# Norm and step sizes in one stage of a Trainium2 kernel, with three projection pieces moved into it from attention

## What is computed

```
h = rmsnorm(x);  P = h @ W_in                       # one projection, split into
q, k, v, z, xbc, dt_f, dt_b, gate_a, gate_s = split(P)
a = W_a( windowed GQA(q, k, v) with QK norm, rotary, a sink logit per head )
s = W_s( gated RMSNorm( bidirectional SSD scan of conv(xbc), step sizes softplus(dt + bias) ) )
x = x + W_o( sigmoid(gate_a) * a + sigmoid(gate_s) * s )
x = x + top-2-of-8 experts in the top-1-of-4 group ( rmsnorm(x) )
```

## Time and profile before

| | us |
|---|---|
| median of 3 runs | 2020.5 |
| lowest, highest | 2015.5, 2022.53 |
| the profiled execution, whole time | 2021.15 |
| its span in the trace | 2019.3 |
| TensorE busy in it | 1816.7 (90%) |
| mean granted TensorE clock | 0.947 of full |

### The profile page before, as it was taken

How to read it: one execution, slowest core, us unless ns; L and a number is a source line. 1 busy time by engine, 2 the same in 40 slices (tenths; PEclk the granted TensorE clock), 3 DMA queues, 4 the chain that set the end, 5 groups by cost and what they waited for, 6 DMA issues and landing times. The chain is left out here.

```text
span 2019.3 us, 26351 instructions
## 1 busy us (share of the span) xinstructions
PE 1816.7 (90%) x9522; PEld 1435.8 (71%) x9522; DVE 1305.0 (65%) x1359; ACT 1021.0 (51%) x1593; POOL 660.7 (33%) x374
## 2 busy tenths in 40 slices
PE   4888998999899989899999898985999999999992
PEld 3777887887778765577778787773677777777771
DVE  2686875884886671734344446315888888888884
ACT  4243533444354343166676422222677777777871
POOL 5147637555764871300034432311010011100100
PEclk7899999999999998899999999886999999999996
DMA  3242433435335343311156463334899999999995
GB/s 112 67 123 81 128 105 98 120 107 146 100 105 142 112 139 143 99 51 58 61 157 195 142 211 107 118 139 151 317 358 371 369 378 366 377 375 371 368 354 197
DMA packets 228111, 379.51 MB, mean 188 GB/s; under 512 B 14576, under 2 KB 176624, under 8 KB 203312
## 3 DMA queue, kind: packets, MB, share of 16 engines
q1 hardware_dynamic: 220272, 363.45, 52.5%
q0 software_dynamic: 7168, 12.60, 1.8%
q10 hardware_dynamic: 576, 2.18, 0.3%
HBM read 333.94 MB, written 55.25 MB: 193 GB/s over the span
## 5 line engine op out<-in xcount | busy, mean ns | idle before, releaser
L2064 DVE TENSOR_TENSOR e_w_low<-e_raw,e_w_high 128x2048 fp32r<-128x2048 f32 x190 | 426.5, 2285 | 62.1 <-ACT e_w_high L2060 62.1
L523 POOL TENSOR_TENSOR w_w_low<-w_raw,w_w_high 128x1024 fp32r<-128x1024 f32 x92 | 252.6, 2746 | 452.1 <-ACT w_w_high L518 452.1
L185 PE MATMUL bank<-h_high,w_w_high 128*128 128x256 f32 x960 | 338.0, 352 | 31.9 <-ACT ssd_conv_in L802 16.7
L2060 ACT ACTIVATE e_w_high<-e_raw 128x2048 fp32r<-128x2048 f32 x190 | 349.7, 1914 | 0.0
L185 PE MATMUL bank<-h_low,w_w_high 128*128 128x256 f32 x960 | 329.0, 343 | 0.0
L185 PE MATMUL bank<-h_high,w_w_low 128*128 128x256 f32 x960 | 328.3, 342 | 0.0
L185 PEld LDWEIGHTS bank<-h_high,w_w_high 128*128 128x128 f32 x960 | 188.1, 196 | 66.4 <-issue 30.7
L2076 PE MATMUL bank<-e_w_high,e_xT_high 128*96 128x512 f32 x512 | 206.6, 404 | 3.2 <-DVE e_xT_low L2157 1.6
L946 DVE SCALAR_TENSOR_TENSOR ssd_xc<-ssd_conv_in,ssd_conv_p,ssd_xc 128x774 f32<-128x774 f32 x144 | 196.3, 1364 | 10.8
L2076 PE MATMUL bank<-e_w_high,e_xT_low 128*96 128x512 f32 x512 | 203.3, 397 | 0.0
L2076 PE MATMUL bank<-e_w_low,e_xT_high 128*96 128x512 f32 x512 | 202.3, 395 | 0.0
(11 more groups left out here) (296 smaller groups left out, 3600.3 us busy)
## 6 DMA issues: line engine op xcount, KB each, us to landing
e_raw<-in_w_gate SPq DMA_DIRECT2D x64, 1024.0 KB, 7.4
e_raw<-in_w_up SPq DMA_DIRECT2D x64, 1024.0 KB, 7.6
e_raw<-in_w_down SPq DMA_DIRECT2D x64, 1024.0 KB, 6.8
w_raw<-in_w_in SPq DMA_DIRECT2D x68, 512.0 KB, 3.9
ssd_decays<-decay_sums SPq DMA_DIRECT2D x48, 512.0 KB, 6.2
projected<-ssd_side SPq DMA_DIRECT2D x36, 384.0 KB, 2.5
w_raw<-in_w_out_ssm SPq DMA_DIRECT2D x16, 512.0 KB, 4.1
y_ssd<-ssd_y SPq DMA_DIRECT2D x24, 256.0 KB, 2.4
```

The costliest lines, as they stand in the source:

```text
L185: last = pe.matmul(out, lhs[k][a], rhs[k][b], start=(k == 0 and m == 0), stop=(k == n - 1 and m == 2))
L523: pool.tensor_tensor(self.pair[u].low[:, :, :], self.raw[u][:, :, :], self.pair[u].high[:, :, :].bitcast(F32), ALU.subtract).then_inc(self ...
L2060: act.activation(pair[n].high[:, :], core.raw[c][:, :], ACT.Copy).then_inc(high_ok, 1)
L2064: dve.tensor_tensor(pair[n].low[:, :], core.raw[c][:, :], pair[n].high[:, :].bitcast(F32), ALU.subtract).then_inc(low_ok, 1)
```

## The change

`norm_and_transpose` and `step_sizes` become one stage, `front`. Three side pieces (`FRONT` = 3, the first three by number) are multiplied in it.

- The piece order begins with these three, then xbc of group 0, and goes on as before: the scan keeps 9 side pieces a group, each three numbers further on. `ATT_SIDES` falls from 8 to 5, so attention has 15 units: nine in the opening, six in the loop.
- SyncE issues six piece loads behind the loads of x and of the step sizes' weights.
- The norm loop: VectorE scales two tiles ahead, not one, and makes the low part of the second half of each tile; GpSimd makes the first half's. The transposes use four banks in turn, not eight. ScalarE rounds the step sizes' weights after tile 0 and one piece after each of tiles 1, 2 and 3. GpSimd makes six pieces' low parts after the loop.
- TensorE: all transposes, the two products of the step sizes (in one bank, the second waits for the copy of the first), the short half of piece 0, the six small transposes, the short halves of pieces 1 and 2, the chunk sums (they wait for the copies of all three short halves), the long half of piece 0, and, after the sums have left their banks, those of pieces 1 and 2.
- `a` is made ahead of the clipped `log_dt`.
- In attention the four stores of zeros go out together after the third side piece, not after the third to sixth.

The core of the diff (what only renumbers pieces in the scan, and the semaphores' names, is left out):

```
-SIDES, LAST_SIDES = 9, 9
-SSD_SIDES = (SG - 1) * SIDES + LAST_SIDES
+FRONT, SIDES, LAST_SIDES = 3, 9, 9
+SSD_SIDES = FRONT + (SG - 1) * SIDES + LAST_SIDES
...
             @block.sync
...
                 sp.dma_start(core.w_dt[:, :, :], core.w_in_cols(DT0, 2 * SH)).then_inc(core.w_dt_in, 16)
+                for n in range(2 * RING):
+                    load_piece(sp, core, n)
+                for n in range(FRONT):
+                    sp.wait_ge(first_left, n + 1)
+                    sp.wait_ge(second_left, n + 1)
+                    sp.dma_start(core.projected[n * P:(n + 1) * P, :], side[n][:, :]).then_inc(side_out, 16)
+                    if n == FRONT - 2:
+                        sp.wait_ge(sumT_ok, 2)
+                        for d in range(2):
+                            sp.dma_start(core.sums[d], sumT[:, d, :]).then_inc(sumT_out, 16)
...
+            @block.tensor
...
+                def steps(s):
+                    if s:
+                        pe.wait_ge(dtT_ok, s)
+                    pe.wait_ge(w_low_ok, 1)
+                    pe.wait_ge(first_low_ok, FIRST[s] + TILES[s])
+                    pe.wait_ge(second_low_ok, FIRST[s] + TILES[s])
+                    products(pe, core.bank[4][0:H2, 0:SEQS[s]], weights, h_parts(core, FIRST[s] * P, SEQS[s]))\
+                        .then_inc(dtT_mm, 1)
...
+                for t in range(NT):
+                    transposes(t)
+                for s in range(2):
+                    steps(s)
+                first(0)
+                for t in range(NT):
...
+                    last = pe.transpose(core.bank[0][:, t * H2:(t + 1) * H2], dtT[:, t * P:(t + 1) * P],
+                                        core.ident[0:H2, 0:H2])
+                last.then_inc(dt_mm, 1)
+                for n in range(1, FRONT):
+                    first(n)
+                pe.wait_ge(a_ok, 1)
+                pe.wait_ge(first_left, FRONT)
...
+                second(0)
+                pe.wait_ge(sumT_ok, 2)
+                for n in range(1, FRONT):
+                    second(n)
...
             @block.scalar
...
+                    if t == 0:
+                        act.wait_ge(core.w_dt_in, 16)
+                        act.activation(w_pair.high[:, :, :], core.w_dt[:, :, :], ACT.Copy).then_inc(w_high_ok, 1)
+                    if 0 < t <= FRONT:
+                        round_piece(act, core, t - 1)
...
             @block.gpsimd
...
-                    for j in range(2):
-                        pool.wait_ge(high_ok, 2 * t + j + 1)
-                        at = (slice(None), slice(4 * j, 4 * j + 4), slice(t * P, (t + 1) * P))
-                        pool.tensor_tensor(core.h.low[at], hT[j][:, :, :], core.h.high[at].bitcast(F32),
-                                           ALU.subtract).then_inc(low_ok, 1)
+                    pool.wait_ge(high_ok, 2 * t + 1)
+                    at = (slice(None), slice(0, 4), slice(t * P, (t + 1) * P))
+                    pool.tensor_tensor(core.h.low[at], hT[0][:, :, :], core.h.high[at].bitcast(F32),
+                                       ALU.subtract).then_inc(first_low_ok, 1)
+                for n in range(2 * FRONT):
+                    lower_piece(pool, core, n)
...
             @block.vector
...
-                scaled(0)
+                for t in range(2):
+                    scaled(t)
                 for t in range(NT):
-                    if t + 1 < NT:
-                        scaled(t + 1)
                     for j in range(2):
...
+                    if t + 2 < NT:
+                        scaled(t + 2)
+                    dve.wait_ge(high_ok, 2 * t + 2)
+                    at = (slice(None), slice(4, 8), slice(t * P, (t + 1) * P))
+                    dve.tensor_tensor(core.h.low[at], hT[1][:, :, :], core.h.high[at].bitcast(F32),
+                                      ALU.subtract).then_inc(second_low_ok, 1)
...
-                    if 2 <= i < 2 + D // ZW:
-                        zeros(i - 2)
+                    if i == 2:
+                        for c in range(D // ZW):
+                            zeros(c)
```

More of the change, by code:

```diff
@@ L222, in refined_root, with front @@
     return dve.tensor_tensor(out, out, part, ALU.mult)
-def norm_and_transpose(core):
+def front(core):
     nc = core.nc
@@ L274, in _ @@
                                        ACT.Copy).then_inc(high_ok, 1)
+                    if t == 0:
[3 more added lines that the diff above has]
+                        round_piece(act, core, t - 1)
+                act.activation(rate[:, :], core.row[:, R_ALOG:R_ALOG + H2], ACT.Exp).then_inc(rate_ok, 1)
+                for s in range(2):
+                    step_parts(s)
+                leave_first(0)
+                act.wait_ge(raw_ok, 1)
+                act.activation(low[:, :, :], low[:, :, :], ACT.Exp)
+                act.drain()
+                act.activation(low[:, :, :], low[:, :, :], ACT.Ln, bias=core.ones[:, 0:1]).then_inc(soft_ok, 1)
+                act.wait_ge(dt_ok, 1)
+                act.activation(tab["log_dt"], tab["log_dt"], ACT.Ln)
+                for n in range(1, FRONT):
+                    leave_first(n)
+                act.wait_ge(exp_in_ok, 1)
+                for name in ("reach", "to_end", "decay"):
+                    last = act.activation(tab[name], tab[name], ACT.Exp)
+                last.then_inc(exp_ok, 1)
+                for n in range(FRONT):
+                    leave_second(n)
             @block.gpsimd
@@ L703, in scan @@
                     store(g, NT - 1)
-                for n in range(RING, GC + 2 * RING):
+                for n in range(2 * RING, FRONT + GC + 2 * RING):
                     load_piece(sp, core, n)
@@ L789, in _ @@
                 pe.sem_inc(y_mm, NT)
-                for n in range(GC):
+                for n in range(FRONT, FRONT + GC):
                     project(n, n % RING)
@@ L850, in scan @@
                             leave_side(g, sides[n], n)
-                act.sem_inc(left, 2)
+                act.sem_inc(left, 2 + 2 * FRONT)
                 act.wait_ge(pads_ok, 1)
                 for ct in range(GC):
-                    leave(ct, ct, ct)
-                    round_piece(act, core, ct + RING)
+                    leave(FRONT + ct, ct, ct)
+                    round_piece(act, core, FRONT + ct + RING)
                     if 0 < ct < GC - 1:
```

238 lines of the change are left out of this document (105 added, 133 removed).

## The result

The changed kernel takes 2026.52 us (median of 20 runs, 2020.38 to 2031.16) against 2020.39 (20 runs) before; the ratio is 1.0021, interval 1.0012 to 1.0031: 4 us slower by 2 to 6. A second comparison, made beside the experiments, gave 1.0014 (0.9999 to 1.0029). The forecast was 2021 us in a range from 2011 to 2029, and no difference beyond 0.3%. The time lies in the range, 5.5 us above the forecast, and the difference is under 0.3%: 3 to 4 us, where the sum of the forecast had 0.3.

A forecast was written before the change was run, and what follows sets the result against it. TensorE, busy for 90% of the span, was taken as the bound, so a change pays where it idles. From 2021.15, +12.5 (front), -15.4 and +3.2 (attention) made 2021.5; forecast 2021 us, range 2011 to 2029.

The forecast's parts named there:

- The norm loop: Front: about 3.0 to 3.6 us a tile without contention; with 0.5 to 1.1 charged, last low part at 35.0.
- The collision: Norm loop: VectorE's and GpSimd's low parts of a tile contend for SBUF, charged 0.5 to 1.1 us a tile.
- the fourth rival: Front: pieces late, norm loop over 3.5 us a tile, short halves misfit; front +17 to +20, 2027 us; chance 0.12.
- The step sizes: Front: bias add at 44.4 us, sums start at 50.5 and take 4.4 at full clock, ending at 54.9.
- the tail: Front, after the last long half: copy, rounding, low part and border, 5.0 us, before the scan's first projection at 76.3.
- The clock fall between the two products: Front, step sizes: a bound, not expected; 2.7 us more if the clock falls there.
- The loop: Attention's loop of 24 groups, g0 to g23: gives back 12.2 us, from -15.4 and +3.2.
- The half-clock groups: Attention's g1 and g2, without a unit until g3: 7.5 us each at half clock; g1 to g3 +3.2 in all.
- The other groups: Attention groups losing a unit or a piece's end, apart from g1 to g3: give back 15.4 us.
- The clock did not come back by itself: Rival, attention: full clock returns in g1 or g2 without a unit, 5 to 8 us less, about 2013; chance 0.18.
- The slower rival: Attention: clock falls in stretches without units, 8 us for one (2029), 2045 and more if in all; chance 0.1.
- the forecast's +12.5 and -12.2: Scan's first projection 12.5 us later, at 76.3 instead of 63.77; attention gives back 12.2 us.

The follow-up runs named there:

- the first unit moved: Changed kernel with the attention loop's first unit in g1 instead of g3: ratio to the kernel before 0.9985, 2018.74 us.
- the low parts moved: Changed kernel with both low parts of a tile on GpSimd again: ratio to the kernel before 1.0009.
- the zeros spread: Changed kernel with the four stores of zeros one by one after attention's second to fifth side piece: ratio to the kernel before 1.0022.
- attention alone: Kernel before with only the change's attention, 5 side pieces and 15 units, three pieces not computed: ratio to the kernel before 0.9936.
- one edit away: Changed kernel with one of the loop's six units moved into the wait at the end of attention's opening: ratio to the kernel before 1.0072.
- the two runs of one side alone: Kernel before with only the change's attention, 0.9936; changed kernel with eight side pieces in attention again, 1.0059; both ratios to the kernel before.

## Why the prediction was right, and where it was off

**The norm loop.** I had the last low part at 35.0 and the second product at 35.1; it began at 34.26. The collision was there, at 1.66 us for VectorE's part against 0.69 with GpSimd idle, and in the shape forecast: GpSimd finishes and VectorE waits for it. The last tile shows it bare: GpSimd's part takes 1.27 us, as alone, and VectorE's, begun 0.55 later, ends 0.55 after it. GpSimd's 1.66 in the tiles before goes with something that I did not have: VectorE's scaling is running when GpSimd's part begins (21.78 to 22.52 against 22.00), and in the last two tiles, where no scaling is left, it takes 1.30 and 1.27. The Trainium skill's sentence on the shared SBUF interfaces (GPSIMD Engine Reference, "Key points") agrees with the rows of the two subtractions. The period was 3.55 us for the tiles with a scaling and 3.19 for the last two; so the first condition of the fourth rival (over 3.5) was met, and its price was not. As a reason against the edit it was sound: the split gained 0.5 to 0.8 us in the traces and nothing that shows in the timed runs.

**The step sizes.** Bias add 44.4 forecast, 43.41 measured; sums at 50.5, 49.88; 4.4 us at full clock, 4.2. (I had read half of the old 6.6 us as at half clock; their mean clock was 0.63, so about 4.9 us were, which makes 4.2.) The long halves took 16.6 us where I had 16.4, and the tail 4.64 where I had 5.0 with the last copy's lag. All terms but the first were within 0.4; the front as a whole was 0.9 too long. The clock fall between the two products, kept as a bound of 2.7 us, happened in two of the other traces (bias add at 45.2 and 45.4), and cost 1.8 to 2.

**The loop.** -12.0 measured, -12.2 forecast, from two errors that cancel. The half-clock groups were priced too low: 7.5 each forecast, 8.59 and 8.24 measured, near the upper bound of 8.6 that I had from twice the work. That it came near the bound is chance: the work did not double. TensorE was busy for 7.59 us of g1 and waited 1.00 for VectorE's maximum. My 7.5 took g0, added 1.5 for what it lacked, and left out the waits: g0 was busy for 5.46, so it lacked 2.1, and waited for 0.23. g3 was 8.91, not 9.73. So the three groups cost +4.2 and not +3.2. The other groups then gave back 16.2 and not 15.4; g6 and g22, priced at 6.0, came at 5.80, and g12 at 6.38 gave back 1.64 as priced.

**The rivals.** The clock did not come back by itself: 30.7 us at half clock in the changed kernel's loop and the scores ahead of it, from 858 to 888.7, of which TensorE was busy for 28.2. The Trainium skill's picture of activity that releases the clock (TensorE: Matmul & The Clock Gate, "What's actually happening") has to be read with this beside it: the clock rose in the unit of g3, and not before. The slower rival, a fall of the clock in the stretches without units, did not show in any trace with the changed kernel's places of the units: its two, and those with the first unit moved, the low parts moved, the zeros spread, and attention alone. It came one edit away, and not by the length of the stretch, which I had named: beside a group in which TensorE waited twice (in two traces, and not in six others with the same waits). The length then set what it cost. The pieces came in time, as the hole of 0.56 us shows.

**The difference that is left.** By the first pair of traces front and loop make -0.4 us. That pair flatters the change: it sets one of the slower traces of the kernel before beside the fastest front of the changed one. Over all traces the scan's first projection is at 63.1 us with the old front (62.1 to 63.9, four traces) and at 76.1 with the new one and its pieces (75.4 to 77.3, six), and the loop takes 164.1 with the old attention (five) and 152.8 with the new (five): +13.0 and -11.3, together +1.7. So the forecast's +12.5 and -12.2 are each within 1 us here too. By the two runs of one side alone 0.9936 x 1.0059 = 0.9995 (from their ends, 0.9957 x 1.0076 and 0.9915 x 1.0042, between 0.9957 and 1.0033), and the change measured 1.0021 and 1.0014. These agree within their intervals, and the middle of them is 1 to 3 us above the +1.7 of the traces. The places where the first pair of traces had it, opening and output stage, do not hold it in the repeated traces, where the opening of the changed kernel is the shorter one (88.0 against 92.2). A fall of the clock in the loop in some executions would be such a cost, but no trace of the changed kernel has one, nor has its loop the meeting of a piece's end and an output that went ahead of the falls seen. What these 1 to 3 us are, if they are more than the spread, stays open.

**The term not asked.** The prediction priced the front as one: +12.5. Priced apart, it would have shown about -6.5 for the fusion and +18 to 19 for the pieces, against 11 to 12 in attention, and with that the better kernel. That forecast and result are both near 0 says nothing of these parts, which are 6.5 us and more each way.

## What to carry to other kernels

When a change fuses two stages and fills the new one with work from elsewhere, price the two apart: here the first was worth 6.5 us and the second lost all of them, 7 us by the stages of the traces and 10 to 11 by the timed runs. Filler is worth what it covers at its new place less what it covered at its old one. Three pieces of 25 us cost 18 in the front, since only their short halves met a hole, and freed 11 to 12 in attention, since units there had been filling waits of TensorE and one of them had brought its clock back. Where dense matmuls are spread among sparse ones, the first should come early: moving one unit by two groups gave 6.9 us in the loop. And a long gap between them makes every fall of the clock dearer.

## What the runs showed of the hardware

- Float32 transposes, scores and value products of attention, with TensorE busy for 28.2 of 30.7 us, did not bring the full clock back in that time; at full clock the same work kept it for three groups (16 to 22 us) in all traces with the changed kernel's places of the units, and for five (25.5 us) with the first unit moved. It was lost, in two other traces, in a group with two waits of TensorE (0.63 and 0.86 us, busy for 6.03 of 7.52; 0.76 and 0.48 us, busy for 4.30 of 5.54), and kept in six other traces beside the same waits (five times 0.63 and 0.86 us, busy for 5.25 of 6.73, once 0.76 and 0.47).
- VectorE and GpSimd each making a 128x512 subtraction from SBUF, GpSimd beginning 0.55 us earlier: GpSimd 1.27 to 1.30 us, as alone; VectorE ends 0.55 us after it and so takes 1.27 to 1.29, against 0.69 alone. With a scaling of VectorE (0.74 us) still running when GpSimd began, GpSimd's took 1.66, and VectorE's subtraction again ended 0.54 to 0.55 us after it.
- The same stages of the same kernel differ by 2.7 us (output stage, mean clock 0.96 and 0.94), 3 us (opening of attention) and 4.5 us (scan) between two executions. A difference of a few us in one stage of two single traces shows nothing; here it would have sent the search to the output stage.
